# A hybrid decoder layer on one core: x rows over two queues, the third scaling on VectorE, the S5 states turned behind the first projection tile

## The chip, the cores and the metric

The kernel runs on one core of a Trainium2 chip. The metric is the device time of one execution in microseconds (us). The kernel before has a median of 1715.67 us over three runs (1713.98 to 1722.49 us).

## The reference

One layer of a decoder is computed for 272 prompt tokens (16 learned meta tokens and 256 real ones) and 64 sample tokens (8 sequences of 8), all in fp32. Cut to its steps:

```
xn   = rmsnorm(x, g_mix)                       # 336 tokens x 2048
proj = xn @ w_in                               # q, k, v, r, a_low, u
o_gla: gated linear attention in chunks, 4 heads, state 128 x 256 each
o_s5 : dt = exp(log_dt); mag = exp(lam_re*dt)
       ab = mag * (cos(lam_im*dt), sin(lam_im*dt))        # complex decay
       f  = ((ab - 1) / lam);  bb = f * b                 # scaled input matrices
       h_t = ab * h_(t-1) + bb u_t,  first step adds ab * h0   # 64 groups x 64 states
       y5 = Re(c h) + d_skip * u;  z = gelu(y5);  o_s5 = z * sigmoid(z @ w_glu + b_glu)
h = h + concat(o_gla, o_s5) @ w_out
h = h + hierarchical MoE(rmsnorm(h)): 32 experts, top 1 group, top 2 experts, SwiGLU, hidden 512
y = rmsnorm(h, g_final); also the new GLA and S5 states
```

## The kernel before

Each engine has its own instruction list, written out by hand, and semaphores tie the lists together. A list is in order: an instruction that waits holds up all behind it on its engine. SyncE (SP), ScalarE (ACT) and GpSimd (POOL) also issue DMAs, each on a queue of its own.

**The norm.** The 336 tokens lie in `xr` as three tiles of 112 rows by 2048. Tile 0 is meta (16 rows) and 96 rows of `x_prompt`, tile 1 is 112 rows of it, tile 2 is 48 rows of it and the 64 rows of `x_sample`. ACT squares a tile and sums its rows (`square`, L869) when its DMAs have landed, VectorE (DVE) forms the mean (L1122), ACT takes the root (L873), DVE the reciprocal (L1124), and the rows are scaled in place: tiles 0 and 2 by DVE (L1128), tile 1 by ACT (L882). TensorE (PE) transposes them in 12 groups of four 112-column transposes (L1683, groups 0 to 3 are tile 0) through four PSUM banks, and DVE multiplies each group by `g_mix` into `xnT` (L1141). PE waits until all 12 are there (`xn_ready` at 12).

**The projections.** PE goes through 37 tiles (`TILES`). A full tile is 16 fp32 matmuls of 336 columns (L1827), each of which the profile shows as two. Weights come in chunks of two tiles (2048 KB) over two `ring` buffers, loaded by SP (`load_chunk`, L466).

**The S5 parameters.** `log_dt`, `lam_re`, `lam_im` and four small vectors are loaded, turned by PE before the x tiles (L1672 to L1676, `prm_turned` at 1) and copied out by ACT (L885, L887). ACT then takes exp for `dt` (L889), and POOL works out the arguments of sine and cosine (to L647, `arg_ready` at 2). The starting states `st_ld` (four transfers, L480) are turned by PE into PSUM bank 7 (L1689, `prm_turned` at 2) behind the twelfth group of x, once all six of the transfers that count on `s5_loaded` (four of states, two of the matrices `b`, L483) have landed. ACT waits for this and copies the states to `h0` (L892); only behind that copy, in ACT's list, stand mag, sine and cosine (L894 to L896, `trig_ready`).

**What hangs on them.** POOL waits for `trig_ready`, works out `f` and the scaled `b` (`pad`, L681, `pad_ready` at 1), then the tables of rotations (`cmul`, to `tables_ready`), then writes the `c` matrices into `pad` (L735, `pad_ready` at 2). PE turns the pads ahead of tiles 3 and 6 (`turn_pad`, L1701). DVE waits for `tables_ready`, expands them (`tables`, L1159 to L1165) and does 32 steps of forward rotation, scan and rotation back (L1177 to L1208); PE feeds it (`s5_in`, L1713) and multiplies by `c` (`s5_out`, L1725), spread over the projection tiles.

**Behind that** come the gates and the GLA chunks, `w_out`, the routing, and the experts, whose weights are streamed by SP in pieces of 2048 KB.

Of the kernel before, what the change touches and what calls it, by code (L numbers as in the profile page):

```python
# [18 lines left out]
ACT = mybir.ActivationFunctionType  # L19
AX = mybir.AxisListType  # L20

D = 2048
# [97 lines left out]
def build(nc, A):  # L120
    ctx = ExitStack()
    with ctx:
# [178 lines left out]
        s5_loaded = sem("s5_loaded")  # L301
        ldt_loaded = sem("ldt_loaded")
        c_loaded = sem("c_loaded")
        masks_made = sem("masks_made")
# [140 lines left out]
        def _(sp):  # L445
            w_in = A["w_in"][0].rearrange("(p k) n -> p k n", k=KT)
            w_glu = A["w_glu"][0].rearrange("(k p) n -> p k n", p=128)
            w_out = A["w_out"][0].rearrange("(k p) n -> p k n", p=128)
            xp, xs = A["x_prompt"][0], A["x_sample"].rearrange("b t d -> (b t) d")

# [16 lines left out]

            sp.dma_start(ldt_ld, A["log_dt"][0].rearrange("(j g) -> j g", g=2)).then_inc(ldt_loaded, 16)
            for r_, name in enumerate(("lam_re", "lam_im")):
                sp.dma_start(lam_ld[:, r_, :], A[name][0].rearrange("(j g) p -> j (g p)", g=2)).then_inc(lam_loaded, 16)  # L470
            sp.dma_start(xr[0:N_META, 0, :], A["meta"]).then_inc(x_loaded[0], 16)
            sp.dma_start(xr[N_META:XT_ROWS, 0, :], xp[0:96, :]).then_inc(x_loaded[0], 16)
            sp.dma_start(xr[:, 1, :], xp[96:208, :]).then_inc(x_loaded[1], 16)
            sp.dma_start(xr[0:48, 2, :], xp[208:256, :]).then_inc(x_loaded[2], 16)
            sp.dma_start(xr[48:112, 2, :], xs).then_inc(x_loaded[2], 16)
            load_chunk(0)
            for r_, name in enumerate(("state_s5_re", "state_s5_im")):
                src = A[name][0].rearrange("b (j g) p -> (b j) (g p)", g=2)
                for m in range(2):
                    sp.dma_start(st_ld[:, 2 * r_ + m, :], src[128 * m:128 * m + 128, :]).then_inc(s5_loaded, 16)  # L480
            for r_, name in enumerate(("s5_b_re", "s5_b_im")):
# [71 lines left out]
        def _(pool):  # L553
# [113 lines left out]

            pool.wait_ge(s5_loaded, 16 * 6)
            tb = Region(arena, at_d + 1344 + 16, 1456)
# [177 lines left out]
        def _(act):  # L847
            sc = nc.scalar
            st = Steps(act, act_steps)

            act.dma_start(gmix, A["g_mix"][0].rearrange("(p k) -> p k", k=KT)).then_inc(gmix_loaded, 16)
            act.dma_start(vec_ld[0:8], A["g_gla"][0].rearrange("h (m p) -> (h m) p", p=128)).then_inc(vec_loaded, 16)
# [13 lines left out]
            def square(t):  # L866
                act.wait_ge(x_loaded[t], (32, 16, 32)[t])
                ejunk = arena[0:XT_ROWS, D * t:D * t + D]
                sc.activation(ejunk, xr[:, t, :], ACT.Square, accum_out=xss[0:XT_ROWS, 0, t:t + 1]).then_inc(xn_sq, 1)  # L869

            def root(t):
                act.wait_ge(xn_mean, t + 1)
                sc.activation(xss[0:XT_ROWS, 0, t:t + 1], xss[0:XT_ROWS, 0, t:t + 1], ACT.Sqrt).then_inc(xn_sqrt, 1)  # L873

            square(0)
            root(0)
            square(1)
            root(1)
            square(2)
            root(2)  # L880
            act.wait_ge(xn_rstd, 2)
            sc.activation(xr[:, 1, :], xr[:, 1, :], ACT.Copy, scale=xss[0:XT_ROWS, 1, 1:2]).then_inc(xn_scaled[1], 1)  # L882

            act.wait_ge(prm_turned, 1)
            sc.activation(prm[:, LR:LDT + 1, :], ps[:, 4, 0:3 * NJ].rearrange("p (a j) -> p a j", a=3), ACT.Copy)\  # L885
              .then_inc(prm_ready, 1)
            sc.activation(vecs, ps[:, 4, 3 * NJ:3 * NJ + 28], ACT.Copy).then_inc(vec_ready, 1)  # L887
            act.wait_ge(prm_ready, 1)
# [227 lines left out]
        def _(dve):  # L1116
# [17 lines left out]
            root_inverse(1)  # L1134
            root_inverse(2)
            scale(2)
            dve.wait_ge(gmix_loaded, 16)
            for n in range(12):
                t, g = n // 4, n % 4
                dve.wait_ge(xn_turned, n + 1)  # L1140
                ve.tensor_tensor(xnT[:, 4 * g:4 * g + 4, XT_ROWS * t:XT_ROWS * t + XT_ROWS],  # L1141
                                 ps[:, XB[n % 4], 0:4 * XT_ROWS].rearrange("p (k t) -> p k t", k=4),
                                 bc(gmix[:, 4 * g:4 * g + 4].unsqueeze(2), 2, XT_ROWS), ALU.mult).then_inc(xn_ready, 1)
# [523 lines left out]
        def _(pe):  # L1667
# [9 lines left out]
            for n in range(12):  # L1677
                t, g = n // 4, n % 4
                pe.wait_ge(xn_scaled[t], 1)
                if n >= 4:  # L1680
                    pe.wait_ge(xn_ready, n - 3)
                for k in range(4):
                    mm = te.transpose(ps[:, XB[n % 4], XT_ROWS * k:XT_ROWS * k + XT_ROWS],  # L1683
                                      xr[:, t, 4 * g + k:D:KT], ident[0:XT_ROWS, 0:XT_ROWS])
                mm.then_inc(xn_turned, 1)
                if n == 11:
                    pe.wait_ge(s5_loaded, 16 * 6)
                    for m in range(4):
                        mm = te.transpose(ps[:, 7, 128 * m:128 * m + 128], st_ld[:, m, :], ident)  # L1689
                    mm.then_inc(prm_turned, 1)  # L1690
            pe.wait_ge(xn_ready, 12)
# [95 lines left out]

            for p, (kind, i) in enumerate(TILES):
                if p == PAD_B_TILE:
                    turn_pad(0)  # L1790
# [308 lines left out]
```

## Time and profile before

| | before |
|---|---|
| median of three runs | 1715.67 us |
| lowest, highest | 1713.98, 1722.49 us |
| profiled execution | 1709.05 us, of which the profile's span is 1707.3 us |
| PE busy | 1349.4 us (79%) |
| DVE, ACT, POOL busy | 583.8, 193.7, 105.6 us |
| mean granted TensorE clock | 0.877 of full speed |

The profile is one execution. Its page gives busy times and the chain of work that ended last; the trace behind it can be asked for single waits, instructions in order of time, and stretches. Starts are counted from the span's start. A busy engine need not be the one that sets the end: that is read from the chain and from what each engine waited for.

### The profile page before, as it was taken

The numbers are of one execution on the slowest core, as the hardware profiler recorded it, in microseconds if no ns is written. First come the engines' busy times: TensorE is split into PE (matmuls) and PEld (weight loads), VectorE is DVE, ScalarE is ACT, GpSimd is POOL, SyncE is SP. The second block draws the span as 40 slices with busy tenths as digits, with TensorE's granted clock in tenths as the row PEclk, the third lists the DMA queues.
The fourth block names the chain that finished last, engine by engine and source line by source line (L and its number), as shares of the span: only waits on it lengthen the run. The fifth ranks groups of instructions, "written<-read, shape, count | busy, mean of one in ns | idle before, by whom it ended". The sixth has DMA issues, their size and how long they took to land.

```text
span 1707.3 us, 17152 instructions
## 1 busy us (share of the span) xinstructions
PE 1349.4 (79%) x6845; PEld 707.1 (41%) x6845; DVE 583.8 (34%) x1029; ACT 193.7 (11%) x428; POOL 105.6 (6%) x250
## 2 busy tenths in 40 slices
PE   5989999899998999586677675765866856766867
PEld 4655555455766888462222221221322212222222
DVE  2099999983344000421121120220211301201214
ACT  3111111114212000200000000000000000000002
POOL 5910000000001100300000000000000000000000
PEclk9989999999999999788787887887877978876878
DMA  8322122224125973249999999999999999999995
GB/s 199 99 82 66 50 79 69 68 81 140 34 99 169 355 304 99 93 175 420 427 428 427 429 427 428 428 429 427 429 422 429 425 428 430 417 428 426 388 429 226
DMA packets 107076, 486.81 MB, mean 285 GB/s; under 512 B 17455, under 2 KB 80059, under 8 KB 80331
## 3 DMA queue, kind: packets, MB, share of 16 engines
q1 hardware_dynamic: 104128, 472.99, 69.3%
q0 software_dynamic: 2688, 12.97, 2.1%
q8 instruction: 42, 0.69, 0.2%
q14 instruction: 18, 0.15, 0.0%
q10 hardware_dynamic: 200, 0.02, 0.0%
HBM read 478.29 MB, written 10.78 MB: 286 GB/s over the span
## 4 chain that ended last, share of the span: by engine, by line
PE 38%; DMA 36%; DVE 15%; issue 4%; POOL 3%; SPq 2%; ACT 2%; DVEq 0%; POOLq 0%; ACTq 0%
DMA arena<-in_w_up 35%; PE ps L2004 10%; PE ps L1827 8%; PE ps L1859 7%; PE ps L1954 3%; PE ps L1863 2%; POOL arena L609 2%; PE ps L1776 2%; PE ps L2043 1%; PE ps L1904 1%; DVE arena L1191 1%; DVE arena L1204 1%; DVE arena L1511 1%; DVE arena L1177 1%; DVE arena L1205 1%
## 5 line engine op out<-in xcount | busy, mean ns | idle before, releaser
L2004 PE MATMUL ps<-arena 128*32 128x512 f32 x2048 | 320.2, 772 | 216.0 <-DMA arena<-in_w_up 214.6
L1827 PE MATMUL ps<-arena 128*128 128x336 f32 (+1 forms) x1152 | 342.4, 454 | 0.2 <-ACT arena L941 0.2
L1827 PEld LDWEIGHTS ps<-arena 128*128 128x128 f32 x1152 | 220.8, 195 | 117.3 <-issue 26.8
L2004 PEld LDWEIGHTS ps<-arena 128*32 128x32 f32 x2048 | 80.4, 136 | 444.8 <-issue 444.3
L2043 PE MATMUL ps<-arena 128*32 128x512 f32 x1024 | 153.6, 754 | 22.2 <-DVE arena L1535 19.1
L1528 DVE COPY arena<-ps 128x512 f32<-128x512 f32 x31 | 21.3, 687 | 391.2 <-PE ps L2004 391.2
L1859 PE MATMUL ps<-arena 128*128 128x256 f32 x512 | 112.6, 381 | 0.5 <-issue 0.5
L1954 PE MATMUL ps<-arena 128*128 128x512 f32 (+3 forms) x192 | 102.9, 665 | 7.4 <-DVE arena L1511 5.6
L1511 DVE TENSOR_TENSOR arena<-arena,ps 128x1024 f32<-128x1024 f32 (+1 forms) x48 | 58.4, 1218 | 143.7 <-PE ps L1954 143.7
L1859 PEld LDWEIGHTS ps<-arena 128*128 128x128 f32 x512 | 96.6, 190 | 14.8 <-issue 1.9
L2043 PEld LDWEIGHTS ps<-arena 128*32 128x32 f32 x1024 | 40.0, 133 | 118.0 <-issue 111.1
L2028 PE MATMUL ps<-arena 128*128 128x64 f32 x256 | 66.4, 404 | 22.8 <-DVE arena L1528 22.0
L1549 DVE COPY arena<-ps 32x512 f32<-32x512 f32 x62 | 42.8, 691 | 120.9 <-PE ps L2043 119.9
L2028 PEld LDWEIGHTS ps<-arena 128*128 128x128 f32 x256 | 62.2, 327 | 41.8 <-DVE arena L1528 40.0
L1052 ACT ACTIVATE arena<-ps 128x128 f32<-128x128 f32 x32 | 8.9, 278 | 553.5 <-PE ps L2028 553.5
L1954 PEld LDWEIGHTS ps<-arena 128*128 128x128 f32 (+3 forms) x192 | 31.3, 182 | 73.8 <-issue 43.1
L1059 ACT ACTIVATE arena<-ps 32x512 f32<-32x512 f32 x62 | 36.4, 587 | 181.9 <-PE ps L2043 181.2
L1713 PE MATMUL ps<-arena 32*128 32x336 f32 x128 | 45.6, 476 | 12.2 <-DVE arena L1178 12.2
L832 POOL DMA_INDIRECT arena<-hn_rows,arena x7 | 7.1, 1012 | 743.8 <-DVE arena L1531 706.3
L1191 DVE TENSOR_TENSOR_SCAN arena<-arena 128x336 f32<-128x336 f32 x64 | 51.4, 845 | 4.2
L1303 DVE SCALAR_TENSOR_TENSOR arena<-arena,ps 128x256 f32<-128x256 f32 x68 | 29.5, 477 | 49.1 <-PE ps L1776 49.1
L1343 DVE TENSOR_TENSOR arena<-arena,ps 128x256 f32<-128x256 f32 x16 | 6.6, 421 | 108.0 <-PE ps L1859 86.4
(342 smaller groups left out, 1072.4 us busy)
## 6 DMA issues: line engine op xcount, KB each, us to landing
arena<-in_w_gate SPq DMA_DIRECT2D x64, 2048.0 KB, 18.4
arena<-in_w_up SPq DMA_DIRECT2D x64, 2048.0 KB, 22.9
arena<-in_w_down SPq DMA_DIRECT2D x64, 2048.0 KB, 22.2
arena<-in_w_in SPq DMA_DIRECT2D x16, 2048.0 KB, 8.9
arena<-in_w_out SPq DMA_DIRECT2D x8, 2048.0 KB, 9.6
arena<-in_state_gla SPq DMA_DIRECT2D x8, 512.0 KB, 8.8
arena<-in_w_glu SPq DMA_DIRECT2D x4, 1024.0 KB, 5.2
out_new_gla_sample<-arena SPq DMA_DIRECT2D x2, 2048.0 KB, 24.2
```

Of the source, the lines that this page charges most:

```text
L609: st(gp.tensor_tensor(o, a, b, ALU.mult))
L1059: sc.activation(Os[CAP * i:CAP * i + CAP, 512 * x:512 * x + 512], ps[CAP * x:CAP * x + CAP, 6 + i % 2, :], ACT.Copy).then_inc(out_a, 1)
L1191: ve.tensor_tensor_scan(Gs[j % 2][:, r_], dec[j % 2], P1[:, r_], 0.0, ALU.mult, ALU.add)\
L1511: ve.tensor_tensor(d_, d_, ps[0:TR[t], b_:b_ + 2, :].rearrange("p b c -> p (b c)"), ALU.add)\
L1549: ve.tensor_copy(Os[CAP * i:CAP * i + CAP, 512 * x:512 * x + 512], ps[CAP * x:CAP * x + CAP, 6 + i % 2, :]).then_inc(out_b, 1)
L1713: te.matmul(ps[:, BU[j % 2][r_], 0:T], BT[rows, r_, c, :], uT[rows, c, :], start=True, stop=True)\
L1827: mm = te.matmul(o, w, x, start=(k == 0), stop=(k == kt - 1))
L1859: mm = te.matmul(ps[:, OB[i % 2][t], 0:256], mixT[:, m, 128 * t:128 * t + 128], w[:, m, :], start=(m == 0), stop=(m == 15))
L1954: mm = te.matmul(ps[0:TR[t], b_ + x, :], Wsel[rows, 128 * t:128 * t + TR[t]], Os[rows, 1024 * j + 512 * x:1024 * j + 512 * x + 512], start ...
L2004: mm = te.matmul(ps[CAP * x:CAP * x + CAP, 0, :], xT[:, 4 * q + at, CAP * i:CAP * i + CAP], wpiece[4 * (q // 2) + 2 * up + q % 2][:, HID * ...
L2028: mm = te.matmul(ps[:, 1, at:at + 2 * CAP], GUs[:, k:HID:4], fold2.rearrange("p x t -> p (x t)"), start=True, stop=True)
L2043: mm = te.matmul(ps[CAP * x:CAP * x + CAP, 6 + i % 2, :], HT[:, k, :], wpiece[8 + k][:, 512 * x:512 * x + 512], start=(k == 0), stop=(k == 3))
```

## The change

Five things are done together.

- **x first, over two queues.** SP issues the three `x_prompt` transfers and then the first weight chunk. ACT's queue takes meta, `log_dt`, `lam_re`, `lam_im` and `x_sample`, ahead of `g_mix` and the four vectors that it had already.
- **DVE scales all three x tiles.** ACT's scaling of tile 1 (L882) is gone. DVE scales tile 1 right behind its reciprocal, and does tile 2's mean, reciprocal and scaling behind the four `g_mix` groups of tile 0.
- **ACT copies the parameters** (two copies) between the root of tile 1 and the square of tile 2, not behind all of them.
- **States apart from b.** The four state transfers count on a semaphore of their own, `st_loaded`; POOL waits for two on `s5_loaded`, not six.
- **The states are turned later in PE's list:** ahead of projection tile 1 (`p == 1`), so behind all matmuls of tile 0, and not behind the last group of x.

```diff
@@ SP
-            sp.dma_start(ldt_ld, A["log_dt"][0].rearrange("(j g) -> j g", g=2)).then_inc(ldt_loaded, 16)
-            for r_, name in enumerate(("lam_re", "lam_im")):
-                sp.dma_start(lam_ld[:, r_, :], A[name][0].rearrange("(j g) p -> j (g p)", g=2)).then_inc(lam_loaded, 16)
-            sp.dma_start(xr[0:N_META, 0, :], A["meta"]).then_inc(x_loaded[0], 16)
             sp.dma_start(xr[N_META:XT_ROWS, 0, :], xp[0:96, :]).then_inc(x_loaded[0], 16)
...
-            sp.dma_start(xr[48:112, 2, :], xs).then_inc(x_loaded[2], 16)
             load_chunk(0)
...
-                    sp.dma_start(st_ld[:, 2 * r_ + m, :], src[128 * m:128 * m + 128, :]).then_inc(s5_loaded, 16)
+                    sp.dma_start(st_ld[:, 2 * r_ + m, :], src[128 * m:128 * m + 128, :]).then_inc(st_loaded, 16)
@@ POOL
-            pool.wait_ge(s5_loaded, 16 * 6)
+            pool.wait_ge(s5_loaded, 16 * 2)
@@ ACT
+            act.dma_start(xr[0:N_META, 0, :], A["meta"]).then_inc(x_loaded[0], 16)
...
+            act.dma_start(xr[48:112, 2, :], xs).then_inc(x_loaded[2], 16)
             act.dma_start(gmix, A["g_mix"][0].rearrange("(p k) -> p k", k=KT)).then_inc(gmix_loaded, 16)
...
-            act.wait_ge(xn_rstd, 2)
-            sc.activation(xr[:, 1, :], xr[:, 1, :], ACT.Copy, scale=xss[0:XT_ROWS, 1, 1:2]).then_inc(xn_scaled[1], 1)
...
+            for t in range(3):
+                square(t)
+                root(t)
+                if t == 1:
+                    act.wait_ge(prm_turned, 1)
...
@@ DVE
             root_inverse(1)
-            root_inverse(2)
-            scale(2)
+            scale(1)
...
+                if n == 4:
+                    root_inverse(2)
+                    scale(2)
@@ PE
-                if n == 11:
-                    pe.wait_ge(s5_loaded, 16 * 6)
-                    for m in range(4):
-                        mm = te.transpose(ps[:, 7, 128 * m:128 * m + 128], st_ld[:, m, :], ident)
-                    mm.then_inc(prm_turned, 1)
...
             for p, (kind, i) in enumerate(TILES):
+                if p == 1:
+                    pe.wait_ge(st_loaded, 16 * 4)
+                    for m in range(4):
+                        mm = te.transpose(ps[:, 7, 128 * m:128 * m + 128], st_ld[:, m, :], ident)
+                    mm.then_inc(prm_turned, 1)
```

PE's list before, from the last x group (L1683) over the states (L1689) to the first projection tiles (L1827):

```order
L1683 MATMUL ps<-arena 128x112 [waits xn_ready,xn_scaled2]
L1683 MATMUL ps<-arena 128x112 x3
L1689 MATMUL ps<-arena 128x128 [waits s5_loaded]
L1689 MATMUL ps<-arena 128x128 x3
L1827 MATMUL ps<-arena 128x336 [waits ring_loaded0,xn_ready]
L1827 MATMUL ps<-arena 128x336 x31
L1827 MATMUL ps<-arena 128x336 [waits ring_loaded1,proj_read]
```

The same place in PE's list now (x groups L1684, states L1788, tiles L1828):

```order
L1684 MATMUL ps<-arena 128x112 [waits xn_ready,xn_scaled2]
L1684 MATMUL ps<-arena 128x112 x3
L1828 MATMUL ps<-arena 128x336 [waits ring_loaded0,xn_ready]
L1828 MATMUL ps<-arena 128x336 x15
L1788 MATMUL ps<-arena 128x128 [waits st_loaded]
L1788 MATMUL ps<-arena 128x128 x3
L1828 MATMUL ps<-arena 128x336 x16
L1828 MATMUL ps<-arena 128x336 [waits ring_loaded1,proj_read]
```

The four state transposes have moved behind the 16 matmuls of tile 0. ACT's list before, from the last square (L869) to cosine (L896), with the copy to `h0` as L892:

```order
L869 ACTIVATE arena<-arena 112x2048 [waits x_loaded2]
L873 ACTIVATE arena<-arena 112x1 [waits xn_mean]
L882 ACTIVATE arena<-arena 112x2048 [waits xn_rstd]
L885 ACTIVATE arena<-ps 128x96 [waits prm_turned]
L887 ACTIVATE arena<-ps 128x28
L889 ACT_TABLE_LOAD
L889 ACTIVATE arena<-arena 128x32 [waits prm_ready]
L892 ACTIVATE arena<-ps 128x512 [waits xn_turned,prm_turned]
L894 ACTIVATE arena<-arena 128x32 [waits arg_ready]
L895 ACT_TABLE_LOAD
L895 ACTIVATE arena<-arena 128x32
L896 ACTIVATE arena<-arena 128x32
```

The same stretch of ACT's list now (squares L873, copies L884 and L886, copy to `h0` L891):

```order
L884 ACTIVATE arena<-ps 128x96 [waits prm_turned]
L886 ACTIVATE arena<-ps 128x28
L873 ACTIVATE arena<-arena 112x2048 [waits xn_sq,x_loaded2]
L877 ACTIVATE arena<-arena 112x1 [waits xn_mean]
L888 ACT_TABLE_LOAD
L888 ACTIVATE arena<-arena 128x32 [waits prm_ready]
L891 ACTIVATE arena<-ps 128x512 [waits xn_turned,prm_turned]
L893 ACTIVATE arena<-arena 128x32 [waits arg_ready]
L894 ACT_TABLE_LOAD
L894 ACTIVATE arena<-arena 128x32
L895 ACTIVATE arena<-arena 128x32
```

The large scaling is out and the copies are ahead of the last square; mag, sine and cosine still stand behind the copy to `h0`. DVE's list now, from tile 1's mean (L1121) over its scaling (L1127) and the `g_mix` groups (L1142) to the last of them:

```order
L1121 TENSOR_SCALAR arena<-arena 112x1 [waits xn_sq]
L1123 RECIPROCAL arena<-arena 112x1 [waits xn_sqrt]
L1127 TENSOR_SCALAR arena<-arena 112x2048 [waits xn_rstd]
L1142 TENSOR_TENSOR arena<-ps,arena 128x4x112 [waits xn_turned,gmix_loaded]
L1142 TENSOR_TENSOR arena<-ps,arena 128x4x112 [waits xn_turned] x3
L1121 TENSOR_SCALAR arena<-arena 112x1 [waits xn_sq]
L1123 RECIPROCAL arena<-arena 112x1 [waits xn_sqrt]
L1127 TENSOR_SCALAR arena<-arena 112x2048 [waits xn_rstd]
L1142 TENSOR_TENSOR arena<-ps,arena 128x4x112 [waits xn_turned] x8
```

Four groups now come ahead of tile 2's scaling and eight behind it, where all twelve were behind it.

## Rows read from the trace of the kernel before

**Rows 1.** The page: the chain that ended last, by engine, then by line.

```profile
PE 38%; DMA 36%; DVE 15%; issue 4%; POOL 3%; SPq 2%; ACT 2%; DVEq 0%; POOLq 0%; ACTq 0%
```

**Rows 2.** That chain in order of time, 0 to 340 us: start, us, what.

```profile
0.79 0.42 SPq L468
...
2.66 0.42 SPq L472
...
18.27 9.88 DMA arena<-in_s_b_im
28.19 0.67 PE ps L1689 x4
28.89 0.60 ACT arena L892
...
81.54 9.00 POOL arena L735 x4
...
339.50 1.36 PE ps L1713 x4
```

**Rows 3.** Waits, whole kernel (PE) and the first 110 us (DVE): us, times, longest.

```profile
DVE arena L1159 <- POOLq L729: 54.1, 1, 54.1
...
PE ps L2004 <- DMA arena<-in_w_up: 214.6, 46, 7.9
```

**Rows 4.** Timeline of the head: start, us, engine, line, operation, idle before.

```profile
2.47 0.43 DVE L1131 COPY arena<-arena 32x128 f32<-32x128 f32 x1 [2.47 <-DMA arena<-in_log_dt]
...
2.88 1.28 ACT L862 ACT_TABLE_LOAD   x1 [2.88 <-issue]
...
8.55 1.91 ACT L869 ACTIVATE arena<-arena 112x2048 f32<-112x2048 f32 x1 [4.18 <-DMA arena<-in_x_prompt]
...
11.21 1.29 DVE L1128 TENSOR_SCALAR arena<-arena 112x2048 f32<-112x2048 f32 x1
...
11.65 1.91 ACT L869 ACTIVATE arena<-arena 112x2048 f32<-112x2048 f32 x1 [0.68 <-DMA arena<-in_x_prompt]
...
16.39 1.91 ACT L869 ACTIVATE arena<-arena 112x2048 f32<-112x2048 f32 x1 [2.31 <-DMA arena<-in_x_sample]
...
20.25 6.77 DVE L1141 TENSOR_TENSOR arena<-ps,arena 128x448 f32<-128x448 f32 x12
...
21.01 5.03 PE L1683 MATMUL ps<-arena 112*128 112x112 f32 x32 [5.21 <-DVE arena L1141]
...
22.24 0.23 ACT L889 ACTIVATE arena<-arena 128x32 f32<-128x32 f32 x1
...
27.99 0.22 POOL L647 TENSOR_SCALAR arena<-arena 128x32 f32<-128x32 f32 x1
...
28.69 27.29 PE L1827 MATMUL ps<-arena 128*128 128x336 f32 x96
...
31.34 0.46 POOL L609 TENSOR_TENSOR arena<-arena 128x32 f32<-128x32 f32 x2 [3.14 <-ACT arena L896]
...
37.93 0.45 ACT L922 ACTIVATE arena<-ps 128x336 f32<-128x336 f32 x1 [6.67 <-PE ps L1827]
...
90.63 3.77 PE L1701 MATMUL ps<-arena 128*128 128x128 f32 x16 [4.27 <-POOLq L738]
```

**Rows 5.** Stretches: start:end, length, busy PE, PEld, DVE, ACT, POOL, clock, DMA share, GB/s.

```profile
11.65:13.50 1.85, 0.95 (x5) 0.95 (x6) 0.84 (x1) 1.85 (x2) 0.00 (x0) 1.00 0.95 146
...
18.00:20.00 2.00, 0.00 (x0) 0.00 (x0) 1.27 (x3) 1.78 (x4) 0.00 (x0) 1.00 1.10 349
...
90.63:94.40 3.77, 3.77 (x17) 3.06 (x17) 3.44 (x8) 1.79 (x3) 0.34 (x2) 0.50 1.04 338
...
98.00:150.00 52.00, 52.00 (x177) 27.84 (x176) 49.85 (x71) 5.02 (x15) 0.00 (x0) 0.95 0.13 41
```

**Rows 6.** DMAs of in_w_in issued in the first 30 us: to landing, min, median, max.

```profile
L466 SPq DMA_DIRECT2D arena<-in_w_in x2: 623/1596/2570, 4.8 to 24.1; - x2
...
DMA to landing us min/median/max: 10.8/14.2/17.6
```

More of the change, by code:

```diff
@@ L302, in build @@
         ldt_loaded = sem("ldt_loaded")
+        st_loaded = sem("st_loaded")
         c_loaded = sem("c_loaded")
@@ L448, in _ @@
             w_out = A["w_out"][0].rearrange("(k p) n -> p k n", p=128)
-            xp, xs = A["x_prompt"][0], A["x_sample"].rearrange("b t d -> (b t) d")
+            xp = A["x_prompt"][0]
             def load_chunk(n):
@@ L849, in _ @@
             st = Steps(act, act_steps)
+            xs = A["x_sample"].rearrange("b t d -> (b t) d")
+            act.dma_start(xr[0:N_META, 0, :], A["meta"]).then_inc(x_loaded[0], 16)
+            act.dma_start(ldt_ld, A["log_dt"][0].rearrange("(j g) -> j g", g=2)).then_inc(ldt_loaded, 16)
+            for r_, name in enumerate(("lam_re", "lam_im")):
+                act.dma_start(lam_ld[:, r_, :], A[name][0].rearrange("(j g) p -> j (g p)", g=2)).then_inc(lam_loaded, 16)
+            act.dma_start(xr[48:112, 2, :], xs).then_inc(x_loaded[2], 16)
             act.dma_start(gmix, A["g_mix"][0].rearrange("(p k) -> p k", k=KT)).then_inc(gmix_loaded, 16)
@@ L867, in square @@
                 act.wait_ge(x_loaded[t], (32, 16, 32)[t])
-                ejunk = arena[0:XT_ROWS, D * t:D * t + D]
+                if t == 2:
+                    act.wait_ge(xn_sq, 1)
+                ejunk = arena[0:XT_ROWS, D * (t % 2):D * (t % 2) + D]
                 sc.activation(ejunk, xr[:, t, :], ACT.Square, accum_out=xss[0:XT_ROWS, 0, t:t + 1]).then_inc(xn_sq, 1)
@@ L873, in root @@
                 sc.activation(xss[0:XT_ROWS, 0, t:t + 1], xss[0:XT_ROWS, 0, t:t + 1], ACT.Sqrt).then_inc(xn_sqrt, 1)
[L875 to L880, printed above, removed]
-            act.wait_ge(xn_rstd, 2)
-            sc.activation(xr[:, 1, :], xr[:, 1, :], ACT.Copy, scale=xss[0:XT_ROWS, 1, 1:2]).then_inc(xn_scaled[1], 1)
[L884 to L887, printed above, removed]
+            for t in range(3):
[3 more added lines that the diff above has]
+                    act.wait_ge(prm_turned, 1)
+                    sc.activation(prm[:, LR:LDT + 1, :], ps[:, 4, 0:3 * NJ].rearrange("p (a j) -> p a j", a=3), ACT.Copy)\
+                      .then_inc(prm_ready, 1)
+                    sc.activation(vecs, ps[:, 4, 3 * NJ:3 * NJ + 28], ACT.Copy).then_inc(vec_ready, 1)
             act.wait_ge(prm_ready, 1)
```

## The prediction

> **What bounds the kernel now.** I read the chain by engine first, then the same chain in order of time, then the waits, and last the timeline of the head. By engine the chain looks like a mix of PE and DMA [rows 1]; the change touches only the first 35 us, so what counts is what the chain does there and whether a shift there reaches the end. In order of time [rows 2] the reader is to see one thread: the last `b` transfer lands, PE turns the states at 28.19, ACT copies them to `h0` at 28.89, mag, sine and cosine follow, and POOL starts again at 31.34 [rows 4]. From there POOL stays on the chain until its last `c` pad, which begins at 81.54 and takes 9.00 us; PE turns that pad at 90.63 [rows 4]. DVE waits 54.1 us for POOL's tables [rows 3] and then hardly rests: 49.85 of 52 us busy in a stretch of the S5 steps [rows 5]. At 339.50 PE takes the chain over [rows 2]. All later stages start from the end of the one before, the weight stream of the experts too, for which PE waits 214.6 us in total [rows 3]. No stage between has slack of its own that I can see, so a shift D of POOL's restart at 31.34 should reach the end one to one. The question is when `trig_ready` comes.
>
> **x over two queues, ahead of the small transfers.** The first `x_prompt` transfer is SP's first issue, at 0.79, and no longer its fifth, at 2.66 [rows 2]: 1.9 us sooner. The tiles are worked on from 8.55, 11.65 and 16.39 [rows 4]. The DMA engines are full in this stretch: share 0.95 at 146 GB/s in the slow part of x, and 1.10 at 349 GB/s when the weight chunk streams [rows 5]. Two queues give no second set of engines in these rows, but `x_sample` (512 KB) now runs beside the first two tiles and delays them, while tile 2 has less left behind them. So the whole of x ends 1.4 to 1.9 us sooner: tile 2 at about 14.7, not 16.39. Tile 0 carries about half of `x_sample` with it and stays at about 8.6, tile 1 comes at about 12.2. Bounds for tile 1: if all x ran at 349 GB/s, the 2.36 MB up to there take 6.7 us; with the issue at 0.79 and the 1.7 us that the smallest transfer took to land (2.47 - 0.79) it comes at 9.2. If the two queues hamper each other, at 13.5 (a third of the slow 146 GB/s stretch more).
>
> The Trainium skill (DMA: Bandwidth & Descriptors, Issuing engines are not separate DMA queues) says that DMAs issued from several engines run on the same 16 DMA engines and interleave, and that only the sequencer's issue time is saved. By that rule the end of x gains the issue time and no more and the total is 1721; by a second queue that carried more, tile 1 comes nearer to 9.2 and the total is 1719. The full shares of the row agree with the rule.
>
> **ACT's side.** Ten issues ahead of its table load instead of five cost it some 2.4 us: five took from 0.79 to the table load at 2.88. Its first work is at 8.55 and it idled 4.18 us before that [rows 4], so tile 0's transfer covers this. The 1.99 us of scaling goes, and the copies go ahead of the last square. Exp for `dt` began at 22.24 and POOL's arguments were done at 28.21 (27.99 + 0.22) [rows 4]; exp now stands behind tile 2's root (at about 18.8 by the next paragraph) and its table load, so at about 20, and the arguments at about 26, 5.97 us behind it as before. Nothing gains from that if the states are later, and they are.
>
> **DVE's side, which sets when tile 0 may start.** Square, mean, root and reciprocal take 11.21 - 8.55 = 2.66 us before the scaling can start [rows 4]. So tile 1, here at 12.2, is scaled from 14.9 and done at 16.2 (1.29 us). Then four groups at 6.77 / 12 = 0.564 us each [rows 4]: 2.26 us, to 18.4. Tile 2's mean, root and reciprocal: about 0.7 us; scaling 1.29: 20.4. Eight groups: 4.51 us. The last is done at 24.9. Before, it was 27.02 (20.25 + 6.77). The first weight chunk landed at 4.8 + 17.6 = 22.4 [rows 6] and comes some 1.5 us sooner: not the limit. PE's projections thus start at 24.9 and not at 28.69, 3.8 us sooner. With tile 1 at 9.2 it would be 21.9, with 13.5 it would be 26.2.
>
> **The states behind tile 0.** What is removed: PE's wait for `b`, which held 28.19. What is added: tile 0 itself. It is 16 matmuls but 32 of the profile's records; 96 records took 27.29 us, so three tiles, 9.1 us each, and ACT's first read-out of a tile comes at 37.93, which is 9.24 us behind 28.69 [rows 4]. So the states are turned at 24.9 + 9.2 = 34.1 and the copy to `h0` starts at 34.8 (0.67 us of transposes [rows 2]). Before: 28.89. D = +5.9 us. The arguments at 26 then wait 9 us in vain, because mag, sine and cosine stand behind the copy in ACT's list. What waits behind that copy: the three activations, hence all of POOL's thread, hence DVE's tables and PE's second pad. ACT's read-out of tile 0 also stands behind them (by 2.5 us) but PE needs it only for tile 2. POOL needs `b` 3 us after its restart, long there.
>
> **What PE gains goes nowhere.** It arrives at the second pad about 3.1 us sooner (3.8 less the 0.67 of transposes) while POOL's pad is 5.9 us later: its wait of 4.27 us [rows 4] becomes about 13 us. After the old wait of 4.27 us the granted clock was 0.50 (1.2 GHz) [rows 5], and DVE did not starve. The longer wait ends at the same low level, so I price it at nothing more; between 0 and 1.9 us, half of the 3.77 that the pad's transposes took there.
>
> **Sum.** D = +5.9 us: the state transposes come behind 9.2 us of tile 0, and the work ahead of them begins 3.3 us sooner (24.9 against 28.19). On the profiled execution: 1709.05 + 5.9 = 1715.0. This execution lies 6.6 us below the median of the runs shown, so I put the same shift on the median: 1715.67 + 5.9 = 1721.6, say 1721. The term's own bounds are +2.9 (tile 1 at 9.2) and +7.2 (at 13.5).
>
> **Rivals.**
>
> *Tile 0 runs at the low clock.* Its start follows x groups that are now paced by DVE: short bursts with a pause of about 2 us for tile 2's scaling and another of 1 us before tile 0. After 4.27 us of idle the clock was 0.50 [rows 5]. If it is at 0.50 during tile 0, its 9.2 us become up to 18.4: D between +6 and +15, total 1722 to 1731. For it: the bursts. Against it: the x groups before were also broken by 5.21 us of idle, and the projections were yet at full speed from 28.69, 9.24 us for the first tile [rows 4]. Chance 0.2. The Trainium skill (TensorE: Matmul & The Clock Gate, Part 4: PE-mode transpose) says that transposes do not count as busy for this clock in the same way. By it tile 0 would start cold in both kernels; the first tile before, at full speed right behind transposes alone, speaks against it.
>
> *The thread is not the end of the chain.* The states may be late without being felt, if DVE or PE has slack that the trace hides: DVE's idle in the S5 stretch is 2 us of 52. Then D is 0 to 3 and the time about 1716 to 1718. Against it: the 54.1 us wait of DVE for POOL and POOL's unbroken thread. Chance 0.08.
>
> *Faster: the parameters were what POOL waited for, and tile 0 is out of the way in time.* The arguments were ready at 28.21, 0.7 us before the copy to `h0` began, so the early copies and the lighter ACT could bring POOL's restart forward to about 26 + 2.4 = 28.4 (2.45 us from copy to restart as before), a gain of 3 us, total 1712.7. The deciding point: tile 0 would have to start before 19.0 (28.89 - 9.9). Even with all x at 349 GB/s DVE's groups end at 21.9. Chance 0.07, most of it for effects that I don't name.
>
> **Chances and range.** Forecast (+2.9 to +7.2) 0.65, cold tile 0 0.2, hidden 0.08, faster 0.07. A measurement of this kernel can tell about 0.5% (8.6 us) from no change; the runs shown spread by that much. The forecast lies below that bound but not far: with scatter a seventh of it reads slower (0.1), with most of the cold cases (0.15) and some of what I missed I put slower at 0.28. Faster by over 0.5% needs -8.6 us, which none of the cases gives: 0.05 for the unnamed. The range from 1713 to 1730 holds the forecast with the scatter of medians, the hidden case and nearly all of the cold one.
>
> **What would show it.** In the changed profile: tile 0's first matmul at 22 to 26; the state transposes at about 34; the copy to `h0` near 34.8 and POOL's restart near 37.2 in place of 31.34; DVE's tables at 87 in place of 81.35; PE's wait before the second pad about 13 us. Wrong would be: tile 0 over in under 5 us, POOL's restart before 31, or the second pad later by 6 us and the end not.

## The result, and the profile after

| | before | after |
|---|---|---|
| median (20 runs each) | 1712.22 us | 1721.92 us |
| lowest, highest | 1705.15, 1722.49 us | 1712.01, 1736.71 us |
| profiled execution | 1709.05 us | 1726.72 us, span 1724.9 us |

The ratio of times is 1.0066, with a 95% interval of 1.0045 to 1.0088: 0.66% slower, or 11.3 us of 1712 (7.7 to 15.1). It is not the quotient of the two medians, which lie 9.7 us apart. That is slower by over 0.5% as measured, though the interval reaches to the other side of that bound. The median lies 0.9 us from the forecast, but only because two errors cancel: the kernel before, at 1712.22 us over 20 runs, is 3.5 us below the median of the three runs that the forecast started from, and the shift of the medians, 9.7 us, was 3.8 us larger than its +5.9. That the number fits is luck. "Within 0.5%" had the larger chance.

The head of the changed kernel in order of time; columns as in [rows 4]:

```profile
0.79 0.42 SPq L469 DMA_DIRECT2D arena<-in_x_prompt  x1
...
7.42 1.91 ACT L873 ACTIVATE arena<-arena 112x2048 f32<-112x2048 f32 x1 [0.18 <-DMA arena<-in_x_prompt]
...
8.76 1.33 DVE L1130 COPY arena<-arena 32x128 f32<-32x128 f32 x1 [8.76 <-DMA arena<-in_log_dt]
...
10.94 1.91 ACT L873 ACTIVATE arena<-arena 112x2048 f32<-112x2048 f32 x1 [0.58 <-DMA arena<-in_x_prompt]
...
13.59 1.29 DVE L1127 TENSOR_SCALAR arena<-arena 112x2048 f32<-112x2048 f32 x1
...
16.72 0.30 PE L1677 MATMUL ps<-arena 28*128 28x28 f32 x1 [3.68 <-DMA arena<-in_b_glu]
...
16.95 5.35 PE L1684 MATMUL ps<-arena 112*128 112x112 f32 x32
...
18.08 2.79 DVE L1142 TENSOR_TENSOR arena<-ps,arena 128x448 f32<-128x448 f32 x4 [3.20 <-PE ps L1684]
...
22.60 4.34 DVE L1142 TENSOR_TENSOR arena<-ps,arena 128x448 f32<-128x448 f32 x8
...
23.36 2.27 PE L1684 MATMUL ps<-arena 112*128 112x112 f32 x16 [1.06 <-DVE arena L1142]
...
26.99 9.31 PE L1828 MATMUL ps<-arena 128*128 128x336 f32 x32 [1.36 <-DVE arena L1142]
...
28.22 0.22 POOL L643 TENSOR_SCALAR arena<-arena 128x32 f32<-128x32 f32 x1
...
36.13 0.60 PE L1788 MATMUL ps<-arena 128*128 128x128 f32 x4
...
36.77 0.60 ACT L891 ACTIVATE arena<-ps 128x512 f32<-128x512 f32 x1 [14.06 <-PE ps L1788]
...
39.23 0.46 POOL L605 TENSOR_TENSOR arena<-arena 128x32 f32<-128x32 f32 x2 [10.79 <-ACT arena L895]
```

The reader is to see two things. At the bottom, POOL has its arguments at 28.44 and then idles 10.79 us for mag, sine and cosine, which stand behind the copy to `h0` at 36.77, which stands behind tile 0: its restart is at 39.23 and not at 31.34 [rows 4], 7.89 us later. Further up, tile 1 is scaled at 13.59, but PE turns no x group before 16.95: its list has the turn of the four vectors (L1677) ahead of them, and `b_glu` was issued by ACT at 5.40 and was only there at 16.72.

The same kernel between 57 and 140 us:

```profile
89.25 1.29 DVE L1160 TENSOR_TENSOR arena<-arena 128x1088 f32<-128x1088 f32 x1 [62.06 <-POOLq L725]
89.44 8.99 POOL L731 TENSOR_SCALAR arena<-arena 128x512 f32<-128x512 f32 x4 [0.28 <-POOL arena L608]
...
98.54 3.77 PE L1697 MATMUL ps<-arena 128*128 128x128 f32 x16 [13.34 <-POOLq L734]
```

POOL's thread takes the shift along unchanged: DVE's tables 7.90 us later (81.35 before), the second pad 7.91 us later (90.63 [rows 4]). In the windows of after (columns as in [rows 5]), tile 0 runs at a granted clock of 1.00 and the pad at 0.50, the level of 1.2 GHz, as before:

```profile
26.99:36.10 9.11, 9.11 (x32) 6.14 (x33) 0.20 (x1) 0.00 (x0) 1.20 (x5) 1.00 1.12 291
98.50:102.30 3.80, 3.76 (x17) 3.06 (x17) 3.47 (x8) 1.79 (x3) 0.34 (x2) 0.50 0.00 0
```

Most of the shift is still there much later. The chain of waits has the first 64 matmuls of the stage of `w_out` at 550.66 in the kernel before

```profile
550.66 14.05 PE ps L1859 x64
```

and at 557.45 in the changed one, 6.8 us later:

```profile
557.45 14.05 PE ps L1860 x64
```

The spans of the two profiled executions, however, lie 17.6 us apart. Most of the rest is one wait. PE's waits in the whole changed kernel (us in total, times, longest):

```profile
PE ps L1925 <- issue: 17.7, 1, 17.7
PE ps L1697 <- POOLq L734: 13.3, 1, 13.3
```

The wait at L1925, near 1570 us, for which the profile names no releaser, took 6.7 us in the kernel before. A second execution of the changed kernel (`after_again`) was profiled for it:

> The changed kernel once more, for a second profile. In its first profile PE waited 17.7 us at the end of the expert loop for nothing that the profile shows, in the kernel before 6.7 us, and in the four variants 5.8 to 8.0 us. Theory: this wait varies by the run and has nothing to do with the change; a second profile shows 6 to 8 us there and a span near 1714. Rival: it belongs to the change, and is again over 12 us.

```profile
PE ps L1925 <- issue: 8.3, 1, 8.3
```

It took 1718.24 us, with a span of 1716.5 (I had 1714), and the same landmarks in the head (39.35, 89.35 and 98.64 in place of 39.23, 89.25 and 98.54). Over the eleven other profiles of this study that wait was between 5.8 and 8.3 us. So the long wait is no steady part of the change, and the second pair of spans is 9.2 us apart. What made it long once stays open.

Further on, landmarks scatter too. In this second execution the stage of `w_out` starts at

```profile
561.42 15.84 PE ps L1860 x64
```

and not at 557.45: the same kernel, with the same head to 0.1 us, is 4.0 us later here, and 10.8 us later than the kernel before. It is a warning: one pair of profiles can be 10 us wide of the mark in its spans and 4 us at a landmark far from the change, while landmarks near the change agree to 0.2 us.

### The profile page after: what moved, and what is told of

Same layout as the page of the kernel before. It is cut to its first block, busy times and chain, and to the rows that moved or that the text cites. A ratio compares the mean times of both kernels' runs of the same rounds, so it can differ in the third digit from the quotient of the medians.

```text
span 1724.9 us, 17153 instructions
## 1 busy us (share of the span) xinstructions
PE 1345.4 (78%) x6845; PEld 704.5 (41%) x6845; DVE 586.2 (34%) x1030; ACT 191.1 (11%) x427; POOL 105.7 (6%) x250
## 4 chain that ended last, share of the span: by engine, by line
PE 37%; DMA 33%; DVE 17%; issue 5%; ACT 1%; SPq 1%; DVEq 0%; POOL 0%; POOLq 0%; ACTq 0%
DMA arena<-in_w_up 32%; PE ps L2005 10%; PE ps L1860 7%; PE ps L1828 6%; PE ps L1955 4%; PE ps L2044 2%; PE ps L1864 2%; PE ps L1772 2%; DVE arena L1192 2%; DVE arena L1512 1%; DVE arena L1205 1%; DVE arena L1178 1%; DVE arena L1179 1%; PE ps L1905 1%; DVE arena L1206 1%
## 5 line engine op out<-in xcount | busy, mean ns | idle before, releaser
L1828 PE MATMUL ps<-arena 128*128 128x336 f32 (+1 forms) x1152 | 339.4, 451 | 1.5 <-DVE arena L1142 1.4
L1828 PEld LDWEIGHTS ps<-arena 128*128 128x128 f32 x1152 | 218.8, 193 | 116.2 <-issue 23.4
L1721 PE MATMUL ps<-arena 128*32 128x320 f32 x128 | 43.7, 466 | 0.0
```

Of the source, the lines that this page charges most:

```text
L1721: mm = te.matmul(ps[cols_, YB[c % 2], 0:TO], CT[:, r_, c, cols_], Q1[j % 2][:, r_, N_META:T], start=(r_ == 0), stop=(r_ == 1))
L1828: mm = te.matmul(o, w, x, start=(k == 0), stop=(k == kt - 1))
```

## The experiments

Each is compared with the kernel before, on its chip. "Tables" is where DVE's L1159 (L1158 or L1160 in others) starts, against 81.35 before. The restart and the tables are from one profile each.

| kernel | POOL restart | tables, shift | ratio, 95% | us by the ratio |
|---|---|---|---|---|
| after | 39.23 | +7.9 | 1.0066 (1.0045 to 1.0088) | +11.3 |
| states early again | 30.70 | -0.7 | 1.0015 (0.9993 to 1.0036) | +2.6 |
| states late alone | 40.03 | +8.7 | 1.0055 (1.0033 to 1.0077) | +9.4 |
| x on one queue | 38.79 | +7.4 | 1.0040 (1.0012 to 1.0068) | +6.8 |
| queues alone | 30.39 | -1.0 | 1.0001 (0.9976 to 1.0027) | +0.2 |
| trigonometry ahead | 30.28 | -1.2 | 0.9983 (0.9965 to 1.0001) | -2.9 |
| small ones ahead | 38.99 | +7.7 | 1.0055 (1.0026 to 1.0084) | +9.4 |
| parameters at once | 22.39 | -6.4 | 0.9983 (0.9960 to 1.0005) | -2.9 |
| b before the chunk | 21.97 | -9.4 | 0.9979 (0.9951 to 1.0008) | -3.6 |

### States early again (e1_states_early)

The changed kernel, with the four state transposes back behind the last x group.

```
                 mm.then_inc(xn_turned, 1)
+                if n == 11:
+                    pe.wait_ge(st_loaded, 16 * 4)      # ... and the four transposes
...
-                if p == 1:                             # the same, before tile 1
```

> The changed kernel with one step undone: the four state transposes stand behind the last group of x again, waiting for the four state transfers alone. Theory (the states behind tile 0 are the loss): the copy to h0 starts at about 26 to 28 and no longer at 36.8, the arguments (done at 28.4) become the limit, POOL starts again at about 30.5 in place of 39.23, and the time falls by 8 to 9 us, to 1 us below the kernel before. Rival (the loss is the x rows and parameters over two queues, which come late): POOL still starts again at 36 or later, and the time stays within 3 us of the changed kernel.

```profile
25.73 0.60 PE L1690 MATMUL ps<-arena 128*128 128x128 f32 x4
26.37 0.60 ACT L891 ACTIVATE arena<-ps 128x512 f32<-128x512 f32 x1 [3.39 <-PE ps L1690]
27.25 14.96 PE L1828 MATMUL ps<-arena 128*128 128x336 f32 x52 [0.92 <-DVE arena L1142]
...
30.70 0.46 POOL L605 TENSOR_TENSOR arena<-arena 128x32 f32<-128x32 f32 x2 [2.01 <-ACT arena L895]
```

The states are turned at 25.73, while PE would wait for DVE's last groups anyway, and cost tile 0 nothing that can be seen: it starts 0.26 us later than in the changed kernel (27.25 against 26.99), but so does everything from the turn of the vectors on (16.99 against 16.72). POOL waits for the trigonometry 2.01 us, not 10.79. The median is 1712.41 us and the ratio 1.0015, with an interval that holds 1 (I had the time 1 us below that of the kernel before): taking one of the five edits back takes the loss back, to within the noise.

### States late alone (e2_states_late_alone)

The kernel before, with only the transposes moved in front of tile 1 (waiting for `s5_loaded` at six, as they did).

> The kernel before with only the state transposes moved behind tile 0 (they still wait for all six transfers, which have landed by then). Theory: tile 0 starts at 27.1, since PE no longer waits for b, and takes 9.2 us; the states are turned at 36.3, POOL starts again at about 39.4, and the time is 8 us above the kernel before, as much as the whole change costs. Rival (two queues): nothing in the queues differs from before, so POOL's restart moves by less than 3 us and the time stays.

```profile
27.79 9.31 PE L1827 MATMUL ps<-arena 128*128 128x336 f32 x32 [0.87 <-DVE arena L1141]
37.57 0.60 ACT L892 ACTIVATE arena<-ps 128x512 f32<-128x512 f32 x1 [14.82 <-PE ps L1787]
40.03 0.47 POOL L609 TENSOR_TENSOR arena<-arena 128x32 f32<-128x32 f32 x2 [11.54 <-ACT arena L896]
```

This edit alone brings the restart to 40.03 and the ratio to 1.0055: it makes the loss by itself. The other four edits together begin tile 0 only 0.8 us sooner than this (26.99 against 27.79).

### x on one queue, queues alone (e3_x_one_queue, e4_queues_alone)

The first is the changed kernel with meta and `x_sample` on SP, x still ahead of everything there; ACT issues the small transfers alone:

```
+            sp.dma_start(xr[0:N_META, 0, :], A["meta"]).then_inc(x_loaded[0], 16)      # first on SP
...
+            sp.dma_start(xr[48:112, 2, :], xs).then_inc(x_loaded[2], 16)               # behind x_prompt
-            act.dma_start(xr[0:N_META, 0, :], A["meta"]).then_inc(x_loaded[0], 16)
...
-            act.dma_start(xr[48:112, 2, :], xs).then_inc(x_loaded[2], 16)
```

> The changed kernel with meta and x_sample back on SP's queue (x still first on it); ACT's queue keeps only the small transfers (log_dt, lam, g_mix, the four vectors). Theory: the small transfers were held up behind x rows in ACT's queue, which delayed the x transposes from 12 to 16.95 and tile 0 from 24.9 to 26.99. Without x rows in that queue the vectors land by about 11, tile 0 starts at 24.5 to 25.5, POOL starts again at 37 to 37.7, and the time is about 2 us below the changed kernel. Rival (two queues bring x in sooner): tiles 1 and 2 come later than 10.9 and 15, and tile 0 starts at 27 or later.

```profile
16.29 0.30 PE L1677 MATMUL ps<-arena 28*128 28x28 f32 x1 [6.59 <-DMA arena<-in_b_glu]
...
26.55 9.31 PE L1828 MATMUL ps<-arena 128*128 128x336 f32 x32 [1.36 <-DVE arena L1142]
```

I missed the vectors: with no x row in ACT's queue they still came at 16.29. So x rows in their own queue are not needed to delay them; what is left is the x rows in the other queue. Tile 0 starts at 26.55, not at 24.5 to 25.5, and the ratio, 1.0040, can't be told from that of the changed kernel.

The second is the kernel before, with the changed kernel's order of DMA issues on SP and ACT and nothing else:

> The kernel before with only the DMA issues of the changed one (x_prompt first on SP; meta, log_dt, lam and x_sample on ACT's queue). Theory: log_dt lands near 8.8 and the vectors near 16.5, so that the x transposes start near 17, but the states' turn still waits for b, which lands 1 to 1.5 us sooner; POOL starts again at 30 to 31.5, and the time is within 1.5 us of the kernel before. Rival (the queues are the loss): POOL starts again 5 us later or more, and the time is 5 us or more above before.

```profile
15.55 1.91 ACT L870 ACTIVATE arena<-arena 112x2048 f32<-112x2048 f32 x1 [1.46 <-DMA arena<-in_x_sample]
...
27.24 0.66 PE L1690 MATMUL ps<-arena 128*128 128x128 f32 x4 [2.19 <-DMA arena<-in_s_b_im]
...
30.39 0.46 POOL L604 TENSOR_TENSOR arena<-arena 128x32 f32<-128x32 f32 x2 [3.02 <-ACT arena L897]
```

Tile 2 is worked on 0.84 us sooner (15.55 against 16.39 [rows 4]) and POOL restarts 0.95 us sooner. The ratio is 1.0001: the two queues neither make the loss nor a gain that can be measured.

### Trigonometry ahead of the copy (e5_trig_first)

The changed kernel, states still behind tile 0, but ACT does mag, sine and cosine ahead of the copy to `h0`:

```
+            act.wait_ge(arg_ready, 2)
+            sc.activation(pr(MAG), pr(X), ACT.Exp).then_inc(trig_ready, 1)
...                                                     # sine, cosine
             act.wait_ge(prm_turned, 2)
             act.wait_ge(xn_turned, 12)
             sc.activation(h0.rearrange("p r b j -> p (r b j)"), ps[:, 7, :], ACT.Copy).then_inc(h0_ready, 1)
```

> The changed kernel with one thing swapped in ACT's list: mag, sine and cosine come ahead of the copy to h0, not behind it. The states are still turned behind tile 0. Theory (the late states cost only because POOL's thread stands behind their copy): the arguments are done at about 28.4, POOL starts again near 30.7, the copy to h0 still comes near 36.8, which is ahead of POOL's need for it near 43, and the time falls by 8 us against the changed kernel, to that of the kernel before. Rival (turning the states in the middle of the projections costs of itself): POOL starts again near 30.7 but PE or POOL waits later on, and the time stays above before by 4 us or more.

```profile
26.83 11.00 PE L1828 MATMUL ps<-arena 128*128 128x336 f32 x32 [1.36 <-DVE arena L1142]
...
30.28 0.46 POOL L605 TENSOR_TENSOR arena<-arena 128x32 f32<-128x32 f32 x2 [2.00 <-ACT arena L892]
...
38.31 0.60 ACT L895 ACTIVATE arena<-ps 128x512 f32<-128x512 f32 x1 [8.11 <-PE ps L1788]
```

The copy is later than in any kernel here (38.31) and no cost of that can be measured: POOL restarts at 30.28, and the median is 1708.80 us against 1710.19, ratio 0.9983, with 1 just inside the interval. So it is not the late states that cost, but what stood behind them in ACT's list. Here tile 0 took 11.00 us and not 9.31; the window over it shows the clock that it was granted (last value but two), a mean of the two levels:

```profile
26.83:37.83 11.00, 11.00 (x34) 7.21 (x35) 0.21 (x1) 1.86 (x4) 8.10 (x20) 0.84 0.97 245
```

### Small ones ahead (e6_small_ones_ahead)

The changed kernel with `log_dt` and the two `lam` first on SP, ahead of x, and on ACT `g_mix` and the vectors ahead of meta and `x_sample`.

> The changed kernel with the small transfers ahead of the x rows on both queues: SP issues log_dt and lam and then x_prompt; ACT's queue takes g_mix and the four vectors and then meta and x_sample. The states are still turned behind tile 0. In the runs so far the vectors landed at 16.3 to 17 wherever x rows were issued from the start, even with no x row in ACT's own queue. Theory (a small transfer takes its turn behind 8 KB rows, piece by piece, so it is late whenever rows are in flight on either queue): the vectors land by 6, the x transposes start at 12 to 13, tile 0 at 24.5 to 25.5, POOL starts again at 37 to 38, and the time is 1 to 2.5 us below the changed kernel. Rival (tile 0's start is set by something else on DVE or in the weight chunk): the vectors are early, but tile 0 starts at 26.5 or later.

```profile
8.11 0.31 PE L1677 MATMUL ps<-arena 28*128 28x28 f32 x1 [3.91 <-DMA arena<-in_b_glu]
...
10.80 1.91 ACT L873 ACTIVATE arena<-arena 112x2048 f32<-112x2048 f32 x1 [5.43 <-DMA arena<-in_meta]
...
26.75 9.31 PE L1828 MATMUL ps<-arena 128*128 128x336 f32 x32 [0.72 <-DVE arena L1142]
```

The vectors are ready 8.6 us sooner than in the changed kernel (8.11), later than I expected, but now meta is the small transfer beside the x rows: ACT waits for it until 10.80, so tile 1 is squared at 14.25 (10.94 in the changed kernel) and DVE's groups start at 18.11, as late as there (18.08). Tile 0 starts at 26.75 all the same, as the rival had it, and the restart is at 38.99, where I had 37 to 38. The ratio, 1.0055, can't be told from that of the changed kernel. So this run doesn't show what the vectors alone cost; the next one does.

### A better version (f1_params_at_once, f1_again, f2_b_before_chunk)

If POOL's restart is the lever, it can be moved forward: the DMA order of before; ACT copies the parameters and takes exp for `dt` ahead of the first square; DVE scales all three tiles, and does the reciprocal that POOL needs ahead of the `g_mix` groups, not behind them; mag, sine and cosine come right behind tile 2's root, ahead of the copy to `h0`; states behind the last x group.

```
+            act.wait_ge(prm_turned, 1)                 # ahead of load_table(ACT.Sqrt) and square(0)
...                                                     # the two copies, then
+            sc.activation(pr(DT), pr(LDT), ACT.Exp).then_inc(dt_ready, 1)
             load_table(ACT.Sqrt)
...
+            dve.wait_ge(arg_ready, 1)                  # ahead of the g_mix groups
+            ve.reciprocal(pr(RDEN), pr(DEN)).then_inc(dt_ready, 1)
```

> A version built on what the runs showed: DMA issues in the order of the kernel before; DVE scales all three x tiles; ACT copies the parameters and takes exp for dt before the first x tile has landed; DVE forms the reciprocal of the denominator before the g_mix groups; mag, sine and cosine directly behind the root of tile 2, ahead of the copy to h0; the states turned behind the last x group, waiting for their own four transfers alone. Theory (POOL's restart shifts the end one to one, until b or PE stops it): POOL starts again near 22.5, waits for b until 28, and works on the pad from 28.1 in place of 34.41; the second pad is turned near 84.5, and the time is 6 us below the kernel before. Rival (some other work takes the place at once): POOL's pad starts at 28 but the end moves by less than 3 us.

```profile
16.28 2.15 DVE L1142 TENSOR_TENSOR arena<-ps,arena 128x448 f32<-128x448 f32 x4
...
22.39 0.46 POOL L610 TENSOR_TENSOR arena<-arena 128x32 f32<-128x32 f32 x2 [4.60 <-ACT arena L890]
...
25.25 17.14 PE L1826 MATMUL ps<-arena 128*128 128x336 f32 x59
...
28.02 2.08 POOL L610 TENSOR_TENSOR arena<-arena 128x512 f32<-128x512 f32 x2 [2.73 <-DMA arena<-in_s_b_im]
```

The restart comes at 22.39, 8.95 us sooner; then `b` holds POOL for 2.73 us, to 28.02, and DVE's tables start at 74.98, 6.4 us sooner. I had put the gain at 6 us. The median is 1706.97 us against 1710.19, ratio 0.9983 (0.9960 to 1.0005). As the interval just reaches 1, it was run again:

> The version with parameters at once, the same kernel again, for a narrower interval: its first rounds gave 0.9983 of before with an interval of 0.9960 to 1.0005. Theory: POOL works on the pad from 28.0 and the S5 steps start 6.4 us sooner than before, so about 0.996 to 0.998. Rival: no gain that can be measured, 1.000.

1708.78 us against 1712.69, ratio 0.9982 (0.9959 to 1.0005). Taken together, if the two are independent, that is 0.9983 with a half-width of 0.0023 / 1.41 = 0.0016: about 3 us faster than before (0.2 to 5.6), and some 14 us faster than the changed kernel. In the profile 6.05 us of the gain is still there at `w_out` (544.61 against 550.66). Where the other 3 us are, or whether they are missing at all, the intervals don't tell.

For the wait on `b` (f2), SP issued states and `b` ahead of the first weight chunk:

> The same with the four states and the two b transfers issued ahead of the first weight chunk. Theory: b lands near 22.5 and POOL works on the pad from 25.5; the first weight chunk lands near 29 and tile 0 starts there, as late as in the kernel before; POOL's second pad is done near 81.5, and from there PE sets the time, its second pad near 86.5. The time is 8 to 9 us below the kernel before and 2 to 3 us below the version with b behind the chunk. Rival (PE's later start takes back what POOL gains): no faster than that version.

```profile
25.04 2.07 POOL L610 TENSOR_TENSOR arena<-arena 128x512 f32<-128x512 f32 x2 [0.17 <-POOL arena L610]
...
29.07 13.28 PE L1826 MATMUL ps<-arena 128*128 128x336 f32 x36 [4.28 <-DMA arena<-in_w_in]
```

POOL no longer waits for `b`, the tables start at 71.97, but now tile 0 waits 4.28 us for its weights and starts at a granted clock of 0.51, close to the level of 1.2 GHz:

```profile
29.07:35.00 5.93, 5.93 (x11) 3.70 (x12) 0.00 (x0) 0.00 (x0) 5.46 (x6) 0.51 1.14 332
```

At the stage of `w_out` f2 is at 547.64, 3.0 us behind f1, with its tables 3.0 us ahead of it. PE has become the later one: POOL is done with the second pad at 81.15, and PE turns it at 89.52 without a wait for POOL. The ratio, 0.9979, is that of f1 within the noise, where I had 2 to 3 us less; the rival was right. In these two runs `b` and the first weight chunk hold each other up: with the chunk first POOL goes on at 28.02 and tile 0 starts at 25.25, with `b` first it is 25.04 and 29.07.

## Why the prediction came out as it did

**The mechanism held.** One thread from the states over ACT's list to POOL, shifted by tile 0: moving the transposes alone makes the loss (e2), moving them back takes it away (e1), and taking the trigonometry out from behind the copy does so too (e5).

**The step that was mis-sized is tile 0's start.** I had 24.9 and it was 26.99. Of the chain of that paragraph, x was on time: tile 1 at 10.94 (I had 12.2), tile 2 ready before 17.28. But I let DVE's four groups follow tile 1's scaling (16.2), and priced the ten DMA issues on ACT at their issue time alone. The four vectors, which PE must turn before any x group, came at 16.72 in place of 5.57, so the groups began at 18.08: +1.9 us, and tile 0 was late by 2.1 us. f1 shows that this was the missing term: there the vectors were turned at 5.20, tile 1 was squared at 12.16 (12.2 forecast), and the four groups, in the same place of DVE's list, began at 16.28 (16.2) and the last of the twelve was done at 25.19 (24.9). All later landmarks are off by just this: states at 36.13 (34.1 forecast), restart 39.23 (37.2), tables 89.25 (87). D was +7.9, above my upper bound of +7.2, since that bound varied only the arrival of x.

**Point by point.** Tile 0's duration: 9.14 us to the state transposes (9.2). `h0` to restart: 2.46 us (2.45). The arguments waited 8.3 us for the copy to start (9); they were at 28.4, not at 26, again because the vectors held the parameter copies and, behind them, tile 2's square (17.28). PE's wait before the second pad: 13.34 us (13). Price of that wait: 3.77 us for the transposes as before, nothing more.

**One to one to the end?** The four kernels with their tables 7.4 to 8.7 us late are 6.8 to 11.3 us slower by the ratio, 9.2 on average (9.2 by their medians too) for a mean shift of 7.9. That fits, with perhaps a microsecond on top; +11.3 itself has 7.7 as its lower end. At the stage of `w_out` the four stand 6.8 to 8.7 us later. But e4, with its tables 1.0 us sooner, is 2.6 us later there (553.21), within the scatter of 4 us seen between two executions of one kernel, so a microsecond more or less can't be followed that far. On the side of gains it is less sure: 6.4 us bring 3, with an interval from nothing to 6.

**The rivals.** *Tile 0 at the low clock*: not in the changed kernel (clock 1.00), but the danger was real: in e5, with the same instructions ahead of it, it took 11.00 us at 0.84, and in f2 its first 5.93 us ran at 0.51. The Trainium skill (TensorE: Matmul & The Clock Gate, Part 4: PE-mode transpose) says that the full clock does not engage for transposes, which don't count as busy the same way. By that rule all first tiles would start low; the traces have it both ways, 9.31 us at 1.00 and 11.00 at 0.84 behind the same transposes, so here it is a risk and not a rule.

The transposes themselves say more. Sixteen of x took 2.27 us at 23.36 in the changed kernel, and in the kernel before, at the start of PE's work on x:

```profile
12.55 3.25 PE L1683 MATMUL ps<-arena 112*128 112x112 f32 x16 [6.68 <-DVE arena L1128]
```

The same instructions ran 1.4 times slower there, though the profile's clock column reads 1.00 there as well [rows 5]. The likeliest reading is that the early ones ran at the lower level and the column doesn't show it, and that in the changed kernel the level had risen by 23.36, with nothing but transposes before it on PE. No run was made to test that. What made e5 fall back to the lower level during tile 0, and the changed kernel not, stays open.

*The thread is not the end*: excluded by e1 and e2. *Faster*: its mechanism does exist, POOL's thread moved forward gains in f1 (e5's gain is not clear of the noise), but there the trigonometry stands ahead of the copy, and the change left it behind.

**The chances.** "Within 0.5%" got 0.67 because a median shift of 5.9 us is 0.34%; as measured, it came out on the other side of the bound, 0.66%. With the vectors priced it would have been 7.9 us or 0.46%, and the chances of same and slower about even.

## What to carry to other kernels

When work is moved later on one engine, follow not what it computes but what stands behind its consumer in that engine's list: the copy of the states could come at 38.31 unnoticed (e5), the three activations behind it passed their delay on in full (+7.9 us at DVE's tables). Small transfers on which an engine waits belong ahead of the large rows, on whichever queue, and all of them: put beside the rows they don't cost their issue time, they come with the large ones. The vectors came at 16.72 beside the rows and at 5.20 ahead of them (f1); with the vectors ahead and meta left beside, nothing was gained (e6). And judge a change of 0.5% by medians of many runs and by the shift of landmarks near the change, not by the spans of two profiles.

## What the runs showed of the hardware that I had not expected

**A second queue is no bypass for small transfers.** From issue to landing, kernel before, all ahead of or beside few x rows (line, queue, KB, median us):

```profile
arena<-in_log_dt SPq DMA_DIRECT2D x1, 0.2 KB, 1.7
arena<-in_g_mix ACTq DMA_DIRECT2D x1, 8.0 KB, 1.8
```

and in the changed kernel, on ACT's queue, beside SP's x rows:

```profile
arena<-in_log_dt ACTq DMA_DIRECT2D x1, 0.2 KB, 7.5
arena<-in_lam_re ACTq DMA_DIRECT2D x1, 16.0 KB, 8.7
arena<-in_g_mix ACTq DMA_DIRECT2D x1, 8.0 KB, 12.3
```

A transfer of 0.2 KB takes 7.5 us, though part of that is `meta`, which stands ahead of it in its queue: in e3, first in a queue of small transfers alone, it took 3.3 us, but `g_mix` still 12.0. In the trace the packets of the two queues are mixed in time: between 8 and 10 us of e3 it has 87 packets of SP's queue and 83 of ACT's. The Trainium skill (DMA: Bandwidth & Descriptors, Queues, rings and completion order) says that each DMA engine takes turns between the queues that have work for it, a whole packet at a time. The mix in the trace agrees with taking turns; the profile doesn't say which engine moved a packet, nor whether what it calls a packet is what the page does, so it doesn't show how many rows of x (8 KB) a small piece waits for. That such waits add up to the 16.29 us of e3 is argued, not shown; no run changed the size of the rows to test it.

**x over two queues is hardly faster.** Tile 2 was ready 0.84 us sooner (e4), less than the 1.9 us by which the first x transfer was issued sooner.
